# Expert stage of a two-layer transformer on one core: two pairs of experts share one result, half of each down product moves behind the next pair's up, and weights are asked for at other points

## What is computed

```python
def _grouped_moe(x, router_w, router_b, w_gate, w_up, w_down):
    ...
    combine = jnp.sum(jax.nn.one_hot(idx, N_EXPERTS, dtype=jnp.float32) * gate[..., None], axis=1).astype(t.dtype)
    y = jnp.zeros_like(t)
    for e in range(N_EXPERTS):
        h = jax.nn.silu(t @ w_gate[e]) * (t @ w_up[e])
        y = y + combine[:, e:e + 1] * (h @ w_down[e])
    return y.reshape(b, s, d)
```

## Time and profile before

| | |
|---|---|
| median of 3 runs | 696.89 us (696.1 to 696.91) |
| the profiled execution | 696.17 us, of which the span of the trace is 694.4 |
| TensorE busy | 666.0 us, 96% |
| VectorE, ScalarE, GpSimd busy | 320.2, 218.8, 141.4 us |
| moved by transfers | 237.74 MB, mean 342 GB/s over the span |

### The profile page before, as it was taken

The page is one execution under the profiler, slowest core; times in us unless marked ns, Lnnn a source line. Parts: engine busy times, 40 slices in busy tenths (PEclk is TensorE's granted clock), DMA queues, the critical chain, the costliest instruction groups (busy, mean ns, idle before and its releaser), DMA issues.

```text
span 694.4 us, 9895 instructions
## 1 busy us (share of the span) xinstructions
PE 666.0 (96%) x3700; PEld 384.2 (55%) x3700; DVE 320.2 (46%) x662; ACT 218.8 (32%) x426; POOL 141.4 (20%) x161
## 2 busy tenths in 40 slices
PE   9999999999999999999989997999999999999993
PEld 6969878664343333435547975866534333343551
DVE  4767745744243232232267466574324324223226
ACT  4658661531112111111157245353111211111112
POOL 0404110062010010100057690006201001010001
PEclk9999999999999999999999999999999999999998
DMA  9990049899999999999997019379999999999992
GB/s 331 364 384 4 0 158 422 344 376 388 421 421 422 420 422 421 419 423 421 409 417 300 2 44 423 146 308 391 386 421 421 420 421 422 420 421 421 421 408 105
DMA packets 42974, 237.74 MB, mean 342 GB/s; under 512 B 3936, under 2 KB 4112, under 8 KB 18864
## 3 DMA queue, kind: packets, MB, share of 16 engines
q1 hardware_dynamic: 41920, 235.36, 83.4%
q10 hardware_dynamic: 576, 1.05, 0.4%
q0 software_dynamic: 432, 0.70, 0.3%
HBM read 236.04 MB, written 1.05 MB: 341 GB/s over the span
## 4 chain that ended last, share of the span: by engine, by line
PE 76%; DMA 7%; SPq 7%; DVE 5%; ACT 4%; issue 1%; DVEq 0%; ACTq 0%
PE psum L601 73%; DMA ring<-in_moe_w_up 4%; SPq L481 4%; DMA ring<-in_diff_w_qkv 3%; SPq L486 2%; PE psum L1097 1%; ACT ring_rounded L1420 1%; DVE ln_stats L1728 1%; SPq L466 1%; PE psum L989 1%; SPq L468 1%; PE psum L937 0%; ACT scratch L1322 0%; DVE psum L1754 0%; DVE small L2023 0%
## 5 line engine op out<-in xcount | busy, mean ns | idle before, releaser
L601 PE MATMUL psum<-ring,work 128*64 128x512 f32 (+2 forms) x1360 | 229.7, 489 | 1.0 <-DMA ring<-in_moe_w_up 0.5
L601 PEld LDWEIGHTS psum<-ring,work 128*64 128x64 f32 (+1 forms) x1360 | 99.6, 138 | 129.4 <-issue 105.6
L601 PE MATMUL psum<-ring,scratch 128*64 128x512 f32 x512 | 116.9, 598 | 0.9 <-ACT scratch L1569 0.9
L2204 DVE TENSOR_TENSOR scratch<-psum,scratch 128x256 f32<-128x256 f32 x32 | 13.6, 425 | 178.1 <-ACT scratch L1565 178.1
L2284 POOL COPY work<-work 128x512 f32 x60 | 37.3, 625 | 286.7 <-PE psum L601 271.7
L1558 ACT ACTIVATE x_T_rounded<-psum,small 128x512 fp32r<-128x512 f32 x64 | 43.8, 688 | 110.0 <-DVE scratch_rounded L2185 90.3
L1565 ACT ACTIVATE scratch<-psum 128x256 f32<-128x256 f32 x32 | 12.3, 384 | 201.0 <-PE psum L601 201.0
L601 PEld LDWEIGHTS psum<-ring,scratch 128*64 128x64 f32 x512 | 33.9, 136 | 67.9 <-issue 65.1
L601 PE MATMUL psum<-ring_rounded 128*128 128x256 f32 (+2 forms) x230 | 66.3, 309 | 0.0
L601 PE MATMUL psum<-x_T_rounded,scratch_rounded 128*128 128x512 f32 x144 | 63.0, 438 | 0.9 <-issue 0.8
L601 PE MATMUL psum<-ring_rounded,x_T_rounded 128*128 128x512 f32 x192 | 60.8, 398 | 0.0
(11 more groups left out here) (279 smaller groups left out, 841.1 us busy)
## 6 DMA issues: line engine op xcount, KB each, us to landing
ring<-in_moe_w_up SPq DMA_DIRECT2D x64, 1024.0 KB, 20.0
ring<-in_moe_w_gate SPq DMA_DIRECT2D x60, 1024.0 KB, 16.9
ring<-in_moe_w_down SPq DMA_DIRECT2D x60, 1024.0 KB, 20.0
ring<-in_diff_w_qkv SPq DMA_DIRECT2D x5, 2048.0 KB, 20.8
ring<-in_diff_w_o SPq DMA_DIRECT2D x1, 4096.0 KB, 19.0
ring<-in_moe_w_down SPq DMA_DIRECT2D x8, 512.0 KB, 23.4
ring<-in_mla_w_o SPq DMA_DIRECT2D x1, 4096.0 KB, 35.1
ring<-in_moe_w_gate SPq DMA_DIRECT2D x4, 768.0 KB, 6.5
```

What stands on the lines that cost most here:

```text
L601: return pe.matmul(dst, lhsT, rhs, start=start, stop=stop, skip_group_check=True)
L2204: dve.tensor_tensor(h_sb, psum[:, 6, FF:2 * FF], act_s, ALU.mult).then_inc(m["h_ready"], 1)
```

## The change

Three things are changed.

**Shared results.** Pair 0 and pair 15 keep a result of their own; pairs 1 and 2, 3 and 4, up to 13 and 14 share one (`SETS` is 9). Both pairs' down products are added in the same banks 4 and 5, and one set of eight sum matmuls follows where two did. In a shared result the rows of the two pairs must not collide: the second pair's experts are swapped left for right (`swapped`, `expert`), the window starts are moved so that both windows fall on the same 64 slots' worth of rows (five more small VectorE operations ahead of `offs_ready`), and the overflow branch is taken when two experts that share rows have over 64 tokens together. The gate weights are now put on h (a `scalar_tensor_tensor` in place of the product) and no longer on the result. The overflow branch itself is written anew.

**Half of each down moved.** From pair 1 to 14 the right half of a pair's down is issued behind the next pair's gate and up. Pair 15's up weights come in three loads of 3, 3 and 2 eighths (`LAST_UP_PARTS`), and its up matmuls wait for each apart.

**Loads asked for at other points.** Four of the loads of pairs 0 and 1 are issued when 10 instead of 12 projections are done, and four of pair 2 (in layer 1 two of pair 1 and two of pair 2) behind the first half of the output product's right part.

The diff, cut to its core (the part of VectorE that places the windows, ScalarE's same reordering and the overflow branch are left out):

```diff
@@ sync
+                load_gate_up(l, i, s, (0,))
+                for part, ks in enumerate(slice(a, b) for a, b in zip((0,) + LAST_UP_PARTS, LAST_UP_PARTS)):
+                    sp.dma_start(slot_pair(s)[:, :, 1, ks, :],
+                                 both_experts(moe_w_up, i).rearrange("e (p k) f -> p e k f", k=KD)[:, :, ks, :])\
+                      .then_inc((*last_up, rings[l][s]["up"])[part], 16)
...
+            sp.wait_ge(*wo_half(1))
             load_down(1, 1, 1)
-            load_pair(1, 2, 2)
+            load_gate_up(1, 2, 2, experts=(1,))
+            sp.wait_ge(*wo_bank(1, TT - 1, 1))
+            load_gate_up(1, 2, 2, experts=(0,))
+            load_down(1, 2, 2)
@@ tensor
+                def down(i, c):
+                    if i % 2 == 1:
+                        pe.wait_ge(*m("y_act", i + c))
+                        pe.wait_ge(*m("y_dve", i + c))
+                    down_half(i % SLOTS, i % 2, c, i % 2 == 1 or i == 0, i % 2 == 0 or i == PAIRS - 1)\
+                        .then_inc(m[("y0_ps", "y_ps")[c]], 1)
...
                         if i == PAIRS - 1:
-                            combine_previous(0)
-                        pe.wait_ge(*rings[l][s]("up", turn * 32))
-                        gate_or_up(1, s, buf).then_inc(m["gu_ps"], 1)
+                            down(i - 1, 1)
+                            combine(SETS - 2, 0)
+                            for part, (a, b) in enumerate(zip((0,) + LAST_UP_PARTS, LAST_UP_PARTS)):
...
+                                last = gate_or_up(1, s, buf, range(a, b))
+                            last.then_inc(m["gu_ps"], 1)
...
-                        combine_previous(0)
+                    elif 1 < i < PAIRS - 1:
+                        down(i - 1, 1)
                         transpose()
-                        combine_previous(1)
+                        combine((i - 1) // 2, 1 - i % 2)
                     pe.wait_ge(*m("ht_sb", i + 1))
...
-                        down(s, (m["y0_ps"], m["y_ps"]))
+                        down(i, 0)
+                        if first:
+                            down(i, 1)
@@ vector
+                        dve.scalar_tensor_tensor(out=h_sb, in0=up, scalar=gate_col, in1=act_s, op0=ALU.mult,
+                                                 op1=ALU.mult).then_inc(m["h_ready"], 1)
```

More of the change, by code:

```diff
@@ L90, with swapped, expert @@
 CONSTS = _at
+def swapped(i):
+    return i >= 2 and i % 2 == 0
+def expert(i, j):
+    return 2 * i + (1 - j if swapped(i) else j)
 def shape_constants():
@@ L389, in build @@
         last_down = sem("last_down")
+        last_up = [sem(f"last_up{n}") for n in range(len(LAST_UP_PARTS) - 1)]
         def gate_loads(i, s):
@@ L1219, in step @@
                         pe.wait_ge(o["g"], n + 1)
-                        combine(0)
-                        combine(1).then_inc(o["free"], 1)
+                        for t in range(TT):
+                            for c in range(2):
+                                last = add_rows(t, c, pick_r)
+                        last.then_inc(o["free"], 1)
                     overflow_steps(pe, step)
@@ L1575, in pair @@
[L1575 to L1583 removed]
+                    if not opening:
+                        act.wait_ge(*m("y_ps", i - 1))
+                    act.copy(hT[b], psum[:, 7, 0:FF].rearrange("p (k c) -> p k c", k=2)).then_inc(m["ht_sb"], 1)
@@ new lines, in moe @@
+                silu(0, True)
+                transposed(0, 0, True)
+                for t in range(TT):
+                    act.wait_ge(*m("row_ps", t + 1))
+                    act.copy(gate_row[:, :, t * P:(t + 1) * P],
+                             psum[:, t, 2 * P:4 * P].rearrange("p (j n) -> p j n", j=2)).then_inc(m["row_sb_a"], 1)
+                act.wait_ge(*m("g_ready", 1))
+                for c in range(2):
+                    act.wait_ge(*m(("y0_ps", "y_ps")[c], 1))
+                    upper_first(c, m["y_act"])
@@ L2223, in moe @@
+                hidden(0)
+                key_rows()
+                weights(0)
+                pick(0)
+                weights(1)
+                for i in range(1, PAIRS, 2):
+                    odd_pair(i)
+                    if i == 3:
+                        scale_shift_half(l, 1)
+                    if i + 1 < PAIRS:
+                        even_pair(i + 1)
+                lower(SETS - 1, 0)
+                lower(SETS - 1, 1)
                 with dve.If(more_windows):
                     o = ov[l]
-                    dve.wait_ge(*m("c_ps", PAIRS))
+                    dve.wait_ge(o["free"], 1)
+                    for t in range(TT):
+                        dve.tensor_scalar(sums[:, t, :], xs[:, t, :], ALPHA, None, ALU.mult)
```

409 lines of the change are left out of this document (239 added, 170 removed).

## The result

| | before | changed |
|---|---|---|
| median | 696.5 us (695.39 to 696.91, 4 runs) | 703.12 us (701.11 to 704.3, 4 runs) |
| profiled execution | 696.17 us, span 694.4 | 704.30 us, span 702.5 |

What follows compares the result with a forecast made beforehand. Transfers were taken to end both layers' expert stages. Layer 0's 1.9 us, layer 1's 3.3 (1.6 late stream, 1.7 last pair) and 0.1 for constants on the profiled 696.17 gave 701.5 us, range 697 to 705.

Steps and rivals of the forecast that it cites:

- What bounds: Expert stages: weight transfers, 14.95 us a pair, end both layers; TensorE needs 12.83, so its savings cannot move the end.
- Fewer sums: Expert stages: a pair costs TensorE some 11.8 us, saving 14 us a layer, all becoming waits of 3.1 us; 0.
- the sum: Total of the forecast's terms: layer 0 1.9 us, layer 1 3.3, constants 0.1, added to the profiled 696.17: 701.5.
- The late ask: Pair 4's down load, asked for at 177.4 and 507.1, makes the weight stream 0.2 us later in layer 0, 1.6 in layer 1.
- The last pair: Second half of pair 14's down, now between pair 15's gate and up: 14.04 us becomes 15.78, 1.74 more.
- the stream: Flow of weight loads up to pair 15's gate weights: forecast later by 0.2 us in layer 0, 1.6 in layer 1.
- Last up in parts: Pair 15's up: TensorE reaches it 1.5 us after all its weights have landed, so gain 0 and cost 0.
- earlier asks: Loads of pairs 0 to 2 asked for sooner: no gain, since pair 0's gate must first free room; 0.
- faster transfers: Rival: resting TensorE lets expert weights load faster; no change in time, chance 0.10, or faster (694.3 at 431 GB/s), chance 0.10.
- Even engines: Rival: an empty queue at pair 4 evens the DMA engines, later landings some 1 us earlier a layer; 699.5, chance 0.12.
- A granted clock under 1 in the stage: Sign of a wrong forecast: TensorE's clock falls in the expert stage's new waits; as a rival 705 us, chance 0.09.

Runs made afterwards that it cites:

- e4: Changed kernel with the downs of pairs 1 and 14 both kept whole, ahead of the next pair's gate and up; 696.4 us, ratio 1.0007 to the kernel before.
- e9: Kernel before with half of pair 8's down weights not loaded (1.05 MB a layer less); 694.0 us, ratio 0.9966 to the kernel before.
- e10: Kernel with only the shared results (downs whole, last up whole, asks as before), half of pair 8's down weights not loaded; 694.6 us, ratio 0.9972.
- e3: Changed kernel with pair 14's down kept whole, ahead of pair 15's gate; 700.0 us, ratio 1.0052 to the kernel before.
- e5: Changed kernel with the loads of pairs 0 to 2 asked for where the kernel before asks; 702.6 us, ratio 1.0091 to the kernel before.
- e6: Changed kernel with pair 15's up weights loaded as all others and waited for once; 702.5 us, ratio 1.0086 to the kernel before.
- e1: The changed kernel run and profiled again, nothing edited; 702.4 us, ratio 1.0082 to the kernel before.
- e12: Changed kernel with the downs of pairs 1 and 14 whole and half of pair 8's down weights not loaded; 692.5 us, ratio 0.9924 to the kernel before.
- e2: Changed kernel with pair 1's down kept whole, ahead of pair 2's gate and up; 698.4 us, ratio 1.0033 to the kernel before.

## Why the prediction was right, and where it wasn't

- **What bounds**: right that TensorE's saving is worth nothing: e4, with pairs of 11.8 us, takes as long as the kernel before. "Both layers end on the transfers already" and "TensorE is the faster of the two" were right for layer 0 and too strong for layer 1: with the transfers 2.5 us shorter, e9 has 1.7 us to gain in layer 0 and 0.1 in layer 1, where both end together.
- **Fewer sums, 11.8 us a pair, 3.1 us of waits**: measured 11.81 (the transposes of neighbouring pairs start at 177.56 and 189.37 in the chain) and 2.87. But the 11.8 was put down to the sums alone. e10 shows 12.96 with them gone and the downs whole: it takes the moved half as well, which covers the wait for h. This didn't touch the sum. Nor did a slip: nine results are added, not eight; its fourteen pairs' saving is that of nine.
- **The late ask**: its time was right: 177.6, and 511.1 less the 4.1 us by which layer 1's stage began later, against 177.4 and 507.1. Mis-sized was the landing. I took 7.3 to 7.4 us after the ask, from a queue that was empty; it took 8.6 and 9.0. By the rows the up weights ahead of it landed only at 178.5 and 513.7, after the ask, so the queue wasn't empty for every engine. But the landing isn't the whole of it: in the layer 1 of e3 and e5 the down weights land 7.3 us after the ask, as forecast, and pair 15's gate weights are no earlier. I had 162.0 us from the ask to those (7.4 and 154.6); it is 162.6 to 163.2. Reckoned from the stage's start they come 0.9 and 2.5 us later than before in the two profiled executions, where I had 0.2 and 1.6. Over all profiles with full weights (mean 194.2 in the kernels with the late ask, 192.5 in the others) it is 1.7 a layer, 3.4 in all against 1.8.
- **The last pair**: 15.8 us forecast from gate's start to the end of down, measured 674.20 to 689.95, 15.75. To the statistics it is 1.4 to 1.5 us more, not 1.74, and this made up for a part of the stream's error; e3 gets 1.6 back. Together the stages grew by 2.3 and 4.0 us in the profiles, where the sum had 1.9 and 3.3.
- **Last up in parts, earlier asks**: 0 and 0, shown by e5 and e6. The queue ran idle before 146 as forecast (66 GB/s) without harm.
- **Not foreseen**: what happened between the stages, 1.6 us of the profiled 8.1, and 0.25 ahead of layer 0's stage, where I had 0.1. In e1 it is nothing on balance (120.7 against 120.6), so it varies from execution to execution.
- **The rivals**: no faster transfers (422 GB/s, as before). Even engines: no later landing came earlier; pair 15's gate weights are late in all ten stages with the late ask. A granted clock under 1 in the stage was one of my signs of being wrong, and it came: 0.96 and 0.97 on average over 250 to 340 and 600 to 650. The forecast was right that it is hidden there: of two waits of 2.87 and 2.88 us above, one is followed by 7.09 us of gate and up and the other by 8.78, which takes from the next wait. Over the eight profiles with moved halves, a stretch at half clock begins in, or within 1.3 us behind, 26 of the 40 waits of over 2.8 us for weights in the stages and none of those of up to 2.0 us; the other six profiles have neither. The Trainium skill (TensorE: Matmul & The Clock Gate, "HAM oscillation — how this bites in real kernels") describes a kernel whose waits for transfers, of some 3 to 5 us, dropped the clock every time; here waits of 2.9 us did so two times in three, and none at pair 15, where the wait is 1.36.

## What to carry to other kernels

When two resources end close together (here 1.7 and 0.1 us could be gained on one alone), work saved on one is worth next to nothing, and an order that helps it can still move what the other waits for: follow each moved instruction to the semaphore that it raises and to the load asked for behind that. Look at the first loads of a stage, where the queue is short, and at what stands behind the last landing. An engine's idle time is room only if what it waits for is the bottleneck; cut the bottleneck by a known amount (e9, e10, e12) to see which idle time is which.

## What the hardware showed

**VectorE held up by GpSimd.** In the norm behind layer 0's stage, VectorE has two products (L1638) of some 0.63 us each. Before, one overlapped GpSimd's product (L2402, to 364.75); in the changed kernel GpSimd's (L2561, to 365.25) was over when they began (start us, us, instruction; before, then changed):

```profile
363.41 2.49 DVE L1638 TENSOR_TENSOR work_rounded<-x_T,ring_rounded 128x512 fp32r<-128x512 f32 x2 [0.48 <-ACT ring_rounded L1258]
...
362.38 2.37 POOL L2402 TENSOR_TENSOR ring_rounded<-ring,work_rounded 128x1024 fp32r<-128x1024 f32 x1
```

```profile
365.94 1.29 DVE L1717 TENSOR_TENSOR work_rounded<-x_T,ring_rounded 128x512 fp32r<-128x512 f32 x2 [0.48 <-ACT ring_rounded L1310]
...
362.88 2.37 POOL L2561 TENSOR_TENSOR ring_rounded<-ring,work_rounded 128x1024 fp32r<-128x1024 f32 x1
```

The 1.2 us are on the chain of waits. The Trainium skill (SBUF — State Buffer, "SBUF: two separate sides") says that a VectorE operation with two inputs in SBUF and a GpSimd one that reads SBUF exclude each other for a whole instruction. The traces agree: from the product's start to the end of GpSimd's it is 1.3 us, and it took 1.2 us longer. So do the others: in seven of the fourteen profiles the first product starts while GpSimd's runs, 0.5 to 1.5 us ahead of its end, and each time it is longer by that stretch less 0.14 us; in the other seven it takes 0.69 us.

**The clock in the attention.** In five of the fourteen profiles (the changed kernel, e1, e3, e6, e12) the granted clock averages 0.87 to 0.93 from 414 to 440, in the others 1.00, at the same waits of 1.1 to 1.5 us, which the kernel before has at full clock too. In the changed kernel, e1 and e6 the time between the stages is 120.7 to 122.2 us, against 119.2 in e2 and e5, which like them had VectorE undisturbed: 1.5 to 3.0 us (e3 and e12, with VectorE held up for 0.8 and 1.3 us, took 121.9 and 122.2). All five have a moved half in most pairs, and so do e2, e4 and e5, which show nothing of it; of the six kernels without moved halves none does. Whether the change has a part in it, and what decides it, wasn't settled.
